# Expert weights in single 4 MB loads between the first and the last pairs

## What is computed

```python
def expert_block(args):
    xblk, e = args
    hid = jax.nn.silu(xblk @ w_gate[e]) * (xblk @ w_up[e])
    return hid @ w_down[e]

yb = lax.map(expert_block, (xb, block_e)).reshape(n_rows, d)
return jnp.zeros_like(h).at[row_tok].add(yb * row_w[:, None])
```

## Time and profile before

| | |
|---|---|
| median of 3 runs | 1931.34 us (1930.67 to 1933.36) |
| profiled execution | 1930.34 us, span 1928.6 us |
| PE busy | 1841.9 us, 96% |
| DVE, ACT busy | 573.1 us (30%), 362.0 us (19%) |
| DMA | 592 MB, mean 307 GB/s |
| expert stages | about 880 to 1334 us and 1464 to 1918 us |
| chain that ended last | PE 73%, DMA 23%, DVE 2% |

### The profile page before, as it was taken

One profiled execution on the slowest core, in us unless ns is written; L12 is line 12 of the kernel. 1 busy time (PEld: TensorE's weight loads), 2 busy tenths in 40 slices (PEclk: granted clock), 3 DMA queues, 4 the chain that ended last, 5 costly groups with the idle time before them and its releaser, 6 DMA issues.

```text
span 1928.6 us, 23014 instructions
## 1 busy us (share of the span) xinstructions
PE 1841.9 (96%) x9422; PEld 1193.9 (62%) x9422; DVE 573.1 (30%) x1298; ACT 362.0 (19%) x809; POOL 12.9 (1%) x27
## 2 busy tenths in 40 slices
PE   8999999999999999999999888889999999988888
PEld 7798888857988888575454333335885444333333
DVE  3279550432755603523111011113223111110112
ACT  3440000322301003423211111112013211110111
POOL 1000000000001000000000000000000000000000
PEclk9999999999999999999999999999999999999999
DMA  9746675532377752138999999999547999999996
GB/s 299 268 175 264 275 306 225 198 119 88 141 313 290 308 196 104 67 115 363 424 428 428 428 429 429 429 428 427 203 153 281 421 428 428 429 429 428 428 429 262
DMA packets 52885, 592.02 MB, mean 307 GB/s; under 512 B 6578, under 2 KB 15034, under 8 KB 17218
## 3 DMA queue, kind: packets, MB, share of 16 engines
q1 hardware_dynamic: 52226, 588.74, 74.7%
q10 hardware_dynamic: 576, 2.10, 0.3%
HBM read 585.34 MB, written 1.05 MB: 304 GB/s over the span
## 4 chain that ended last, share of the span: by engine, by line
PE 73%; DMA 23%; DVE 2%; ACT 1%; issue 1%; SPq 0%; DVEq 0%
PE ps L495 27%; PE ps L1193 13%; DMA ring<-in_w_gate 11%; DMA ring<-in_w_up 10%; PE ps L736 8%; PE ps L1302 5%; PE ps L1154 3%; PE ps L1147 2%; PE ps L565 2%; PE ps L782 1%; DMA ring<-in_w_down 1%; PE ps L654 1%; PE ps L583 1%; PE ps L597 1%; PE ps L943 1%; PE ps L1356 1%
## 5 line engine op out<-in xcount | busy, mean ns | idle before, releaser
L1193 PE MATMUL ps<-ring,work 128*64 128x512 f32 x2048 | 458.5, 595 | 59.7 <-DMA ring<-in_w_up 38.2
L495 PE MATMUL ps<-hsq,ring 128*128 128x256 f32 x2048 | 447.3, 380 | 0.8 <-DVE hsq L2018 0.8
L495 PEld LDWEIGHTS ps<-hsq,ring 128*128 128x128 f32 x2048 | 387.8, 190 | 59.5 <-issue 7.0
L1193 PEld LDWEIGHTS ps<-ring,work 128*64 128x64 f32 x2048 | 146.5, 137 | 359.8 <-issue 300.4
L1585 ACT ACTIVATE work<-ps 128x512 f32<-128x512 f32 (+2 forms) x175 | 89.7, 517 | 844.3 <-PE ps L495 324.8
L1302 PE MATMUL ps<-ring,work 128*64 128x512 f32 x992 | 220.0, 595 | 1.7 <-DVE work L2505 1.6
L1302 PEld LDWEIGHTS ps<-ring,work 128*64 128x64 f32 x992 | 68.5, 137 | 135.0 <-issue 130.9
L736 PE MATMUL ps<-work,ring 128*128 128x256 f32 (+1 forms) x704 | 148.6, 373 | 0.0
L1963 DVE SCALAR_TENSOR_TENSOR work<-ring,silu_c,work 128x512 f32<-128x512 f32 x196 | 144.1, 755 | 5.1
L736 PEld LDWEIGHTS ps<-work,ring 128*128 128x128 f32 x704 | 130.5, 190 | 18.7 <-issue 1.7
L2457 DVE TENSOR_TENSOR work<-ps,work 128x512 f32<-128x512 f32 x26 | 18.0, 691 | 405.2 <-ACT work L1585 405.2
(11 more groups left out here) (326 smaller groups left out, 1233.4 us busy)
## 6 DMA issues: line engine op xcount, KB each, us to landing
ring<-in_w_gate SPq DMA_DIRECT2D x64, 2048.0 KB, 20.5
ring<-in_w_up SPq DMA_DIRECT2D x64, 2048.0 KB, 20.7
ring<-in_w_down SPq DMA_DIRECT2D x62, 2048.0 KB, 22.7
ring<-in_w_ada SPq DMA_DIRECT2D x24, 2048.0 KB, 8.5
ring<-in_w_ff_gate SPq DMA_DIRECT2D x10, 2048.0 KB, 13.3
ring<-in_w_ff_up SPq DMA_DIRECT2D x10, 2048.0 KB, 13.3
ring<-in_w_ff_down SPq DMA_DIRECT2D x8, 2048.0 KB, 13.8
ring<-in_ml_w_in SPq DMA_DIRECT2D x6, 2048.0 KB, 10.8
```

What stands on the lines that cost most here:

```text
L495: last = mm(ps[:, b, 0:T], w[:, k, m * P:(m + 1) * P], rhs[:, k, :], start=(i == 0), stop=(i == nk - 1))
L1193: last = mm(ps[e * CAP:(e + 1) * CAP, w, :], xg[:, k, e * CAP:(e + 1) * CAP], row_tile(first, w, e, k), start=(k == 0), stop=(k == last_k) ...
```

## The change

- Gate and up of pairs 2 to 14 and down of pairs 3 to 14 are requested as one load each: 4 MB, 32 KB a partition, into both slots of the matrix at once. That makes 38 loads of 4 MB a layer out of 76 of 2 MB.
- For this the arrays are laid out in HBM with both halves of a partition side by side: `[l, pair]` is 128 x 8192 floats in one run. For down the halves are in exchanged order from pair 1 on, so that `c` = 1 goes to slot 0.
- Gate and up of pairs 0, 1 and 15, down of 0, 2 and 15, and the one half of down 1 remain loads of 2 MB. A half's rows are 16 KB as before, taken at a stride of 32 KB.
- A whole matrix counts on the semaphore of its first slot. PE waits for it once, ahead of its first use; for halves it waits as before. `ROW_HALVES` and `DOWN_HALVES` hold the pairs that are in halves.
- SP requests a whole down at `down_done`. Requests at `half_done` remain for pairs 1 and 15.
- In the branch that isn't run, pair 2 is written out and the loop is one pair shorter.

```diff
 ROWS = 2 * T
 BLOCKS = ROWS // P
 BIG = 1e30
+ROW_HALVES = (0, 1, NEXP // 2 - 1)
+DOWN_HALVES = (0, 2, NEXP // 2 - 1)
 LRU_C = 8.0
@@ -407,7 +409,7 @@
             for first in moe_first:
                 if 0 <= n - first < 3 * NEXP:
                     pair, w, part = (n - first) // RING, (n - first) % RING // 2, (n - first) % 2
-                    return int(w < 2 or part == 0 or pair != 1)
+                    return int(part == 0 or pair in (DOWN_HALVES if w == 2 else ROW_HALVES))
             return n != unused
...
@@ -1162,7 +1164,10 @@
             def rows_arrived(first, w, i, part):
 
                 n = first + 2 * w + part
-                pe.wait_ge(slot_loaded[n % RING], landed(n) + 16 * i)
+                if part == 0:
+                    pe.wait_ge(slot_loaded[n % RING], landed(n) + 16 * i)
+                elif isinstance(i, int) and i in ROW_HALVES:
+                    pe.wait_ge(slot_loaded[n % RING], landed(n) + 16 * ROW_HALVES.index(i))
 
@@ -1173,11 +1178,14 @@
             def down_arrived(first, i, c):
 
                 slot = down_place(i, c)
+                n = first + 4 + (slot or 0)
                 if slot is None:
                     pe.wait_ge(piece_loaded[2], START_DMAS[2] + 16 * EARLY_DMAS * (1 + moe_first.index(first)))
+                elif slot == 1 and isinstance(i, int) and i in DOWN_HALVES:
+                    pe.wait_ge(slot_loaded[n % RING], landed(n) + 16 * DOWN_HALVES.index(i))
                 else:
-                    pe.wait_ge(slot_loaded[(first + 4 + slot) % RING], landed(first + 4 + slot) + 16 * (i - slot) if not isinstance(i, int) or i > 1
-                               else landed(first + 4 + slot) + 16 * i)
+                    n = first + 4
+                    pe.wait_ge(slot_loaded[n % RING], landed(n) + 16 * i)
...
@@ -1234,8 +1242,9 @@
 
                 pair_of_all(0)
                 pair_of_all(1)
-                with pe.Fori(0, NEXP // 2 - 3) as n:
-                    pair_of_all(n + 2)
+                pair_of_all(2)
+                with pe.Fori(0, NEXP // 2 - 4) as n:
+                    pair_of_all(n + 3)
                 pair_of_all(NEXP // 2 - 1)
...
@@ -1410,31 +1419,30 @@
                 first, e_ = moe_first[l], E[l]
                 weights = [a["w_gate"], a["w_up"], a["w_down"]]
 
-                def load_rows(w, pair, part):
+                def load_half(w, pair, part):
 
                     s = (first + 2 * w + part) % RING
-                    sp.dma_start(ring[:, s, :], weights[w][l, pair, part]).then_inc(slot_loaded[s], 16)
+                    sp.dma_start(ring[:, s, :], weights[w][l, pair][:, part * SLOT:(part + 1) * SLOT]).then_inc(slot_loaded[s], 16)
 
                 def load_pair(w, pair):
 
-                    for part in range(2):
-                        load_rows(w, pair, part)
-
-                def load_down(slot, pair, c):
-
-                    s = (first + 4 + slot) % RING
-                    sp.dma_start(ring[:, s, :], weights[2][l, pair, c]).then_inc(slot_loaded[s], 16)
-
-                early = weights[2][l, 1, 0]
+                    s = (first + 2 * w) % RING
+                    if isinstance(pair, int) and pair in (DOWN_HALVES if w == 2 else ROW_HALVES):
+                        for part in (1, 0) if w == 2 else (0, 1):
+                            load_half(w, pair, part)
+                    else:
+                        sp.dma_start(ring[:, s:s + 2, :].rearrange("p e c -> p (e c)"), weights[w][l, pair]).then_inc(slot_loaded[s], 16)
+
+                early = weights[2][l, 1][:, SLOT:2 * SLOT]
                 for w in range(2):
...
                 def pairs_of_gathered_tokens():
@@ -1479,35 +1488,30 @@
                     freed = e_["gate_full"], e_["up_full"], e_["down_done"]
                     for part, half_freed in enumerate((e_["gate_half"], e_["gate_full"])):
                         sp.wait_ge(half_freed, 1)
-                        load_rows(0, 1, part)
+                        load_half(0, 1, part)
                     sp.wait_ge(e_["up_full"], 1)
                     load_pair(1, 1)
                     sp.wait_ge(e_["half_done"], 1)
-                    load_down(0, 1, 1)
+                    load_half(2, 1, 0)
                     sp.wait_ge(e_["down_done"], 1)
-                    load_down(1, 2, 0)
+                    load_half(2, 2, 1)
                     for w in range(2):
                         sp.wait_ge(freed[w], 2)
                         load_pair(w, 2)
                     sp.wait_ge(e_["down_done"], 2)
-                    load_down(0, 2, 1)
-
-                    def later_down(pair):
-                        sp.wait_ge(e_["half_done"], pair)
-                        load_down(1, pair, 0)
-                        sp.wait_ge(e_["down_done"], pair)
-                        load_down(0, pair, 1)
-
+                    load_half(2, 2, 0)
                     with sp.Fori(0, NEXP // 2 - 4) as i:
-                        for w in range(2):
+                        for w in range(3):
                             sp.wait_ge(freed[w], i + 3)
                             load_pair(w, i + 3)
-                        later_down(i + 3)
                     last = NEXP // 2 - 1
                     for w in range(2):
                         sp.wait_ge(freed[w], last)
                         load_pair(w, last)
-                    later_down(last)
+                    sp.wait_ge(e_["half_done"], last)
+                    load_half(2, last, 1)
+                    sp.wait_ge(e_["down_done"], last)
+                    load_half(2, last, 0)
                     next_layer(lambda w, e: (freed[w], NEXP // 2))
...
     arrays["w_odd_out"] = tiled(g["w_out_odd_2"][0])
     for name in ("gate", "up"):
         w = g[f"w_{name}_2"].reshape(2, NEXP // 2, 2, 2, KT // 2, P, EH)
-        arrays[f"w_{name}"] = np.ascontiguousarray(w.transpose(0, 1, 3, 5, 2, 4, 6)).reshape(2, NEXP // 2, 2, P, SLOT)
+        arrays[f"w_{name}"] = np.ascontiguousarray(w.transpose(0, 1, 5, 3, 2, 4, 6)).reshape(2, NEXP // 2, P, 2 * SLOT)
     w = g["w_down_2"].reshape(2, NEXP // 2, 2, HTL, P, 2, CH)
-    arrays["w_down"] = np.ascontiguousarray(w.transpose(0, 1, 5, 4, 2, 3, 6)).reshape(2, NEXP // 2, 2, P, SLOT)
+    w = w.transpose(0, 1, 4, 5, 2, 3, 6)
+    arrays["w_down"] = np.concatenate([w[:, 0:1], w[:, 1:, :, ::-1]], 1).reshape(2, NEXP // 2, P, 2 * SLOT)
```

More of the change, by code:

```diff
@@ L1431, in load_experts @@
                         sp.wait_ge(*released[first + 2 * w + part - RING])
-                        load_rows(w, 0, part)
+                        load_half(w, 0, part)
                 sp.dma_start(early_con, early[:, HTL * CH:(HTL + 2) * CH]).then_inc(piece_loaded[2], 16)
@@ L1436, in load_experts @@
                     sp.wait_ge(*released[first + 4 + c - RING])
-                    load_down(c, 0, c)
+                    load_half(2, 0, c)
                 sp.dma_start(early_work, early[:, 0:HTL * CH]).then_inc(piece_loaded[2], 16)
@@ L1464, in pairs_of_all_tokens, with pair_of_all @@
                     sp.wait_ge(e_["down_done"], 2)
-                    load_down(0, 1, 1)
[L1466 to L1474, removed]
+                    load_half(2, 1, 0)
+                    def pair_of_all(pair):
+                        gate_and_up_of(pair)
+                        sp.wait_ge(e_["down_done"], 2 * pair)
+                        load_pair(2, pair)
+                    pair_of_all(2)
+                    with sp.Fori(0, NEXP // 2 - 4) as i:
+                        pair_of_all(i + 3)
+                    pair_of_all(NEXP // 2 - 1)
                     next_layer(lambda w, e: (freed[w][0], freed[w][1] * NEXP // 2))
```

## The result

| | before | after |
|---|---|---|
| median | 1931.67 us (17 runs, 1928.49 to 1936.62) | 1934.73 us (17 runs, 1932.78 to 1939.93) |
| profiled execution | 1930.34 us, span 1928.6 | 1934.62 us, span 1932.8 |
| packets of the DMA queue | 52885 | 41941 |
| PE busy | 1841.9 us | 1852.5 us |

The ratio is 1.0019, with a 95% interval of 1.0013 to 1.0026: the changed kernel is 3.1 us slower by the medians, 3.7 us by the ratio. The forecast was +1.4 us, the range 1926.0 to 1939.0.

What follows compares the result with a forecast made beforehand. The prediction took the DMA queue to bound the expert stages from the second pair on. Fewer packets -5.6, thin queue +3.7 and stage end +3.3 gave +1.4 us on 1931.34, so 1932.7 us, range 1926.0 to 1939.0.

Steps and rivals of the forecast that it cites:

- Bound: Expert stages from the second pair on: the DMA queue sets the pace, 29.36 us a pair against PE's 25.3 us.
- Term 1: Steady loads of gate, up and down: fewer packets save 0.076 us per 4 MB load, -5.6 us in all.
- (a): Whole-matrix loads: rows are cut at 16 KB again, so 1937 us, slower; chance 0.18.
- (c): Whole-matrix loads: longer pieces run at the pure rate, all 0.149 us saved, so 1926.6 us; chance 0.16.
- (d): Weight reads in HBM: twice the stride is slower in memory, so 1940 us or above; chance 0.08.
- (e): Full queue: a load's start costs 0.15 us or more unseen in packet durations, so below 1926 us; chance 0.03.
- Term 2: Early pairs 3 to 5: down requested whole at `down_done` lets the queue nearly run dry, +3.7 us, range 0 to 5.
- (b): Early pairs: the thin queue costs nothing, since a load can start within 3 us, so 1929 us; chance 0.10.
- Term 3: End of each expert stage: PE waiting for whole matrices ends the last gate later, +3.3 us, range 2 to 4.
- The clock stays as it is: PE's clock in the loop: no change despite longer gaps, since PE still works 25 of 29 us.
- The fixed cost per DMA: Loads in a full queue: the skill's 2.0 us per DMA would give 148 us less; the prediction said the trace disagrees.

Runs made afterwards that it cites:

- e_cut: Changed kernel with the old layout in HBM: same 4 MB requests and waits, but each partition's row comes as two 16 KB pieces; +7.5 us against the kernel before.
- e_early: Changed kernel with down of pairs 3, 4 and 5 in halves, the first requested at `half_done`; +1.0 us against the kernel before.
- e_late: Kernel before, with the first half of down requested only at `down_done` in pairs 3 to 14; ratio 1.0020.
- e_both: Changed kernel with all of pair 14 and down of pairs 3 to 5 in halves; measured twice, -3.9 and -1.0 us against the kernel before.
- e_last: Changed kernel with pair 14 loaded and waited for in halves as well; -0.4 us against the kernel before.
- e_wait: Kernel before with all its requests, but PE waits for both halves (gate, up of pairs 2 to 14, down of 3 to 14); ratio 1.0031.
- e_stride: Kernel before with the changed kernel's layout in HBM, all halves read at a stride of 32 KB; ratio 0.9998.

## Why the prediction was right, and where not

- **Bound: right.** The queue sets the pace of the loop before and after.
- **Term 1, -5.6 us: right.** A row is one packet; two landings are 9.71 us apart against 9.787, 0.075 us saved for each 4 MB, where 0.076 stood; the steady stretch is 3.4 us shorter over 44 of them, 0.077 each. `e_cut` gives back all but 0.1 us of that. Only the split was off: the marks, reckoned at 8.4 ns each like a row's packet, saved almost nothing, and the rows' packets a little more. Rivals (a), (c), (d) and (e) fall: no cut, no vanished intercept, no price for the stride, none for a load.
- **Term 2, +3.7 us: the mechanism was right, the size good only to a microsecond or two.** `e_early` gives 4.2 and `e_late` 2.6 us, and `e_both` against `e_last` 2.0 (1.5 and 0.5 for the packets); by A of the changed kernel (804.8 + 5.5 for its 74 loads, against 806.0) it is 4.3. The step that failed is the depth of the queue: it was read off the old landings, though the load ahead also had changed its moment (2.0 us left instead of 3.6). By pair the loss was 1.8 and 0.3 us in layer 0 (1.0 and 0.5 forecast), 2.0 and 0.1 in layer 1 (1.2 and 1.0). Rival (b) falls. Up of pair 5 landed 0.9 and 0.7 us late too, which nothing forecast; in layer 0 the DMA view from 1010 to 1024 us has one packet of an instruction queue among 213 others, and a load has landed only with the last of its 16 marks. That this packet is the cause is only argued. Over the fourteen profiles, 37 of the 38 landings that came more than 0.3 us late behind a queue of over 5 us had a 16 KB packet of an instruction queue inside them; but of all 165 loads that had one, 111 were less than 0.1 us late.
- **Term 3, +3.3 us: right.** B grew by exactly 3.3 us, from 87.9 to 91.2. The last gate ended 1897.72 - 1872.56 = 25.2 us after PE's start on up 14, the sum in the prediction has 1895.3 - 1870.13 = 25.2.
- **"The clock stays as it is": wrong.** The sentence looked at the share of time in which PE works, 25 of 29 us. But the changed pair has one wait of 2.2 to 2.7 us where it had several of at most 1.3, and behind such a wait the clock was at 1.2 GHz for 3.4 us, every second pair. In the loop the pace is the queue's, and the steady stretch is as long with eight dips as with none. In the last two pairs a dip costs 1.7 us; the profile of the changed kernel has none there, while four of the six stages of `e_wait`, `e_cut` and `e_early`, which wait for all of pair 14 as it does, have one (both of `e_wait`, layer 0 of `e_cut`, layer 1 of `e_early`). That this mistake left the forecast near the result is luck: with a dip in each end the stages would stand at +6.0 in place of +2.6. How often it happens in unprofiled runs of the changed kernel is open.
- **The sum.** +1.4 forecast, +2.6 in the profiled stages (the 1.2 more are all in A: 0.6 is term 2, 0.1 term 1, and 0.5 is that A of the kernel before, 805.5, itself lies under the 806.0 of its like), +3.1 by the medians. The last 0.5 us is less than what the rest of the kernel scatters. The ratio of 1.0019 is within the 0.2% that stood for no change; its interval goes on to 1.0026.
- **The fixed cost per DMA.** The Trainium skill (DMA: Bandwidth & Descriptors, Anatomy of one DMA) gives the 2.0 us that the prediction quotes for DMAs issued from GpSimd; these loads are issued from SP. No number of the sum goes by it.

## What to carry to other kernels

When a queue of loads sets the pace, count packets: here each had a price that a full queue didn't hide, 3.4 us over 44 loads of 4 MB. But a larger load also frees its buffer later and is usable later, and here both were paid, at the start and at the end of the stage. Keep loads small in the first pairs, where the queue is thin, and in the last two, where PE is the bound. Ask of each wait not only who hides it, but how long it is in one piece: here the clock fell at waits of 2.0 to 2.8 us, and at none of 1.3.

When an effect is smaller than the scatter of the whole, look for a stretch that repeats: medians that scatter by 3 us couldn't say what the dips in the loop cost, and landings that repeat within 0.1 us could.

## What the runs showed of the hardware

- A packet costs some 150.6 ns for each 4 KB plus 8.4 ns, fitted at 4 to 12 KB. The fit holds to 1% up to 32 KB: the views of 1100 to 1200 us give (1.006 x 16 x 100 us - 321 x 9 ns) / 2613 = 615 ns for 16 KB before (fit 611) and (1.001 x 16 x 100 us - 161 x 9 ns) / 1315 = 1217 ns for 32 KB after (fit 1213). The Trainium skill (DMA: Bandwidth & Descriptors, Why small descriptors are slow) names a fixed overhead per packet of about 3 cycles and speaks of it as a penalty of small descriptors. Whether that is what is seen here, no run shows; but going from 16 to 32 KB was worth 0.8% here.
- A wait of PE of 2.2 to 2.7 us in each pair brought 3.4 us at a granted clock of 1.2 GHz about every 58 us, though PE was busy 88% of the stretch. All 67 dips in the expert stages of the profiles began at the end of a wait of 2.0 to 2.8 us or at most 1.4 us behind it; with four matmuls on zeros in the wait it stayed at 2.4 GHz. In the kernels whose waits in the loop were at most 1.3 us (before, `e_stride`, `e_late`) it stayed there too, with PE busy 85 to 86% of the stretch (1100 to 1150 us).
- The granted clock also differed between executions of the same code where PE had no long wait by design (1.00 and 0.83 over the same 20 us around 410 us); in the second the first expert stage began 3.9 us later.
